# The tanh that ends a state convolution, written into the convolution's PSUM bank instead of an SBUF tile

## What is computed

```
z, xbc, dt_raw, q, k, v, g_ssd, g_att = split_cols(u @ w_in.astype(u.dtype), IN_WIDTHS)
xbc = jax.nn.silu(causal_dwconv(xbc, conv_w, conv_b))
xs, bm, cm = split_cols(xbc, (SSD_INNER, SSD_GROUPS * SSD_STATE, SSD_GROUPS * SSD_STATE))
...
lmat = jnp.exp(jnp.where(causal, cs_t[..., :, None] - cs_t[..., None, :], -jnp.inf))
cb = jnp.einsum('bclgn,bcsgn->bcgls', cc, bc)
y_diag = jnp.einsum('bcgls,bcgrls,bcsgrp->bclgrp', cb, lmat, xdt)
```

## Time and profile before

| | |
|---|---|
| median of 3 runs | 1600.13 us (1599.84 to 1602.13) |
| the profiled execution | 1600.18 us |
| its span, first to last instruction | 1598.4 us |
| TensorE busy | 1579.8 us, 99% |
| VectorE busy | 1130.6 us, 71% |
| ScalarE busy | 921.4 us, 58% |
| GpSimd busy | 153.7 us, 10% |

### The profile page before, as it was taken

How to read it: one execution, slowest core, us unless ns; L and a number is a source line. 1 busy time by engine, 2 the same in 40 slices (tenths; PEclk the granted TensorE clock), 3 DMA queues, 4 the chain that set the end, 5 groups by cost and what they waited for, 6 DMA issues and landing times.

```text
span 1598.4 us, 31022 instructions
## 1 busy us (share of the span) xinstructions
PE 1579.8 (99%) x12570; PEld 1542.4 (96%) x12570; DVE 1130.6 (71%) x2416; ACT 921.4 (58%) x1988; POOL 153.7 (10%) x162
## 2 busy tenths in 40 slices
PE   9999999999999999999999999999999999999998
PEld 9999999999999999999999999999999999999986
DVE  7554578787655888557458875597549997888862
ACT  5444356475443765447557544466776887567653
POOL 4000000000000000000000000102343752100000
PEclk9999999999999999999999999999999999999999
DMA  9554555555555555564265555654354335555551
GB/s 290 178 172 158 185 171 164 180 159 172 165 172 183 172 173 178 173 196 141 82 198 165 179 176 185 189 170 133 109 182 144 121 122 170 172 185 185 185 184 53
DMA packets 251390, 266.52 MB, mean 167 GB/s; under 512 B 4763, under 2 KB 246753, under 8 KB 251248
## 3 DMA queue, kind: packets, MB, share of 16 engines
q1 hardware_dynamic: 249600, 260.72, 51.2%
q0 software_dynamic: 1648, 3.81, 0.9%
HBM read 263.42 MB, written 1.09 MB: 165 GB/s over the span
## 4 chain that ended last, share of the span: by engine, by line
PE 85%; DVE 8%; ACT 5%; issue 1%; DMA 0%; SPq 0%; DVEq 0%; ACTq 0%
PE ps L1023 51%; PE ps L1025 25%; DVE wl L2188 3%; ACT wh L1482 1%; PE ps L988 1%; PE ps L986 1%; PE ps L987 1%; PE ps L778 1%; DVE CY L2154 0%; PE ps L763 0%; DVE CY L2276 0%; ACT YH L1328 0%; PE ps L796 0%; DVE R L1808 0%; DVE YB L2166 0%
## 5 line engine op out<-in xcount | busy, mean ns | idle before, releaser
L2188 DVE TENSOR_TENSOR wl<-raw,wh 128x512 fp32r<-128x512 f32 (+1 forms) x968 | 643.8, 715 | 277.0 <-ACT wh L1482 271.3
L1482 ACT ACTIVATE wh<-raw 128x512 fp32r<-128x512 f32 (+1 forms) x1004 | 551.4, 611 | 198.8 <-PE ps L1023 172.9
L1023 PE MATMUL ps<-XH,wh 128*128 128x258 f32 (+3 forms) x2464 | 617.0, 287 | 4.8 <-ACT XH L1118 3.5
L1025 PE MATMUL ps<-XH,wl 128*128 128x258 f32 (+3 forms) x2464 | 613.8, 285 | 0.0
L1023 PEld LDWEIGHTS ps<-XH,wh 128*128 128x128 f32 x2464 | 465.9, 189 | 8.4 <-issue 5.7
L1025 PEld LDWEIGHTS ps<-XH,wl 128*128 128x128 f32 x2464 | 465.2, 189 | 0.1
L1023 PE MATMUL ps<-XL,wh 128*128 128x258 f32 (+3 forms) x2464 | 333.7, 287 | 0.6 <-DVE XL L1891 0.6
L1023 PEld LDWEIGHTS ps<-XL,wh 128*128 128x128 f32 x2464 | 315.1, 189 | 1.8 <-DVE XL L1891 1.3
L1025 PE MATMUL ps<-HH,wl 128*128 128x272 f32 (+1 forms) x704 | 173.4, 284 | 0.0
L1023 PE MATMUL ps<-HH,wh 128*128 128x272 f32 (+1 forms) x704 | 173.4, 285 | 0.0
L1025 PEld LDWEIGHTS ps<-HH,wl 128*128 128x128 f32 x704 | 132.5, 188 | 0.0
(11 more groups left out here) (444 smaller groups left out, 2038.0 us busy)
## 6 DMA issues: line engine op xcount, KB each, us to landing
raw<-in_ffn_wg SPq DMA_DIRECT2D x44, 1024.0 KB, 5.4
raw<-in_ffn_wu SPq DMA_DIRECT2D x44, 1024.0 KB, 5.4
raw<-in_w_in SPq DMA_DIRECT2D x33, 1024.0 KB, 5.3
raw<-in_ffn_wd SPq DMA_DIRECT2D x32, 1024.0 KB, 5.2
raw<-in_w_ffn_in SPq DMA_DIRECT2D x22, 1024.0 KB, 5.1
raw<-in_ffn_wd SPq DMA_DIRECT2D x16, 768.0 KB, 4.6
raw<-in_conv_w_in SPq DMA_DIRECT2D x12, 1024.0 KB, 5.1
raw<-in_w_ffn_out SPq DMA_DIRECT2D x11, 1024.0 KB, 5.0
```

Of the source, the lines that this page charges most:

```text
L1023: mm = e.matmul(o, hi[:, k, c], xk, start=begin, stop=stop)
L1025: e.matmul(o, lo[:, k, c], xk, start=False, stop=False)
L1482: e.activation(wh[u.n % NH][:, c], raw[u.n % NR][:, c], ACT.Copy).then_inc(s_hi, 1)
L2188: e.tensor_tensor(wl[u.n % NR][:, c], raw[u.n % NR][:, c], wh[u.n % NH][:, c].bitcast(F32), ALU.subtract).then_inc(s_lo, 1)
```

## The change

For the eight groups xs (q from 4 to 11) the tanh goes into the PSUM bank of the group's own convolution, and the conv end reads it from there; q from 0 to 3 keep `TH`. The banks of xs j are therefore free only after the conv end: `free` names `s_cz` in place of `s_ctap`. ACT's wait for a free `TH` buffer is gone for these groups. On ACT, the tanh of xs j + 1 moves to the front of its even head step, ahead of EX; on DVE, the conv end moves up by two places in its step.

```diff
--- before.py
+++ after.py
@@ -558,7 +558,7 @@
     gs_after = (6,)
     mixed = []
     for j in range(8):
-        P.group(("xs", j), W_IN, KD, X_0 + 256 * j, 2, two(s_ctap, 6 * (4 + j) + 4))
+        P.group(("xs", j), W_IN, KD, X_0 + 256 * j, 2, two(s_cz, 2 * (4 + j)))
         mixed.append(("xs", j))
         if j == 0:
             P.drain("cb")
@@ -614,6 +614,9 @@
     x_hid = [Xs(HH[f], HL[f], s_hh, s_hl, 22 * f, n0, T) for f, n0 in enumerate((0, 0, NMETA, NMETA))]
     x_ch, x_o = Xs(CH, CL, s_ch, s_cl, 0, 0, T), Xs(OH, OL, s_oh, s_ol, 0, NMETA, T)
     x_a, x_y = Xs(AH, AL, s_ah, s_al, 0, 0, NV), Xs(YH, YL, s_yh, s_yl, 0, 0, NV)
+
+    def conv_bank(q, m):
+        return TH[q % 2][:, m, :] if q < 4 else PS[groups["xs", q - 4].b0 + m][:, 0:T]
 
     def src3(ps, n, sl=None):
         return ps.rearrange("p (a c) -> p a c", a=n)
@@ -1298,11 +1301,11 @@
     def act_conv_end(e, q):
 
         dst = [BC[:, 2 * q + m, :] for m in range(2)] if q < 4 else [CY[(q - 4) % 4][:, m, :] for m in range(2)]
-        if q > 1:
+        if 1 < q < 4:
             e.wait_ge(s_cz, 2 * (q - 2) + 2)
         for m in range(2):
             e.wait_ge(s_ctap, 6 * q + 4 + m + 1)
-            e.activation(TH[q % 2][:, m, :], dst[m], ACT.Tanh, scale=0.5).then_inc(s_th, 1)
+            e.activation(conv_bank(q, m), dst[m], ACT.Tanh, scale=0.5).then_inc(s_th, 1)
 
     def act_gn(e, g, step):
 
@@ -1411,6 +1414,8 @@
 
     def act_heads(e):
         for c in range(16):
+            if c % 2 == 0 and c < 14:
+                act_conv_end(e, 5 + c // 2)
             yield
             E = EX[c % 2]
             if c > 1:
@@ -1424,10 +1429,7 @@
             e.wait_ge(s_er, c + 1)
             e.activation(E[:], E[:], ACT.Exp, scale=-1.0).then_inc(s_ee, 1)
             yield
-            if c % 2 == 0 and c < 14:
-                act_conv_end(e, 5 + c // 2)
-                yield
-                yield
+            yield from idle(2 * (c % 2 == 0 and c < 14))
             if c > 6:
                 if c != 14:
                     act_gn(e, (c - 7) // 4, (c - 7) % 4)
@@ -2100,11 +2102,11 @@
                             DTT[:, :, 2 * c:2 * c + 2].unsqueeze(3).to_broadcast([128, 3, 2, 64]),
                             ALU.mult).then_inc(s_xd, 1)
             yield
-            yield from idle(c % 2 == 0 and c < 14)
-            yield
             if c % 2 == 0 and c < 14:
                 dve_conv_end(e, 5 + c // 2)
                 yield
+            yield
+            yield from idle(c % 2 == 0 and c < 14)
             if c > 6:
                 if (c - 7) % 4 == 2:
                     dve_gn_add(e, (c - 7) // 4)
@@ -2151,7 +2153,7 @@
         dst = [BC[:, 2 * q + m, :] for m in range(2)] if q < 4 else [CY[(q - 4) % 4][:, m, :] for m in range(2)]
         for m in range(2):
             e.wait_ge(s_th, 2 * q + m + 1)
-            e.scalar_tensor_tensor(out=dst[m], in0=TH[q % 2][:, m, :], scalar=1.0, in1=dst[m], op0=ALU.add,
+            e.scalar_tensor_tensor(out=dst[m], in0=conv_bank(q, m), scalar=1.0, in1=dst[m], op0=ALU.add,
                                    op1=ALU.mult).then_inc(s_cz, 1)
 
     def dve_gn_add(e, g):
```

## The result

The changed kernel takes **1605.21 us** (median of 7 runs, 1603.89 to 1607.03), the kernel before 1600.32 (7 runs, 1599.84 to 1602.13) on the same chip: ratio 1.003, 95% interval 1.002 to 1.0039, which leaves out no change. The span of the profiled execution is 1603.6 us, 5.2 more than before's.

A forecast was written before the change was run, and what follows sets the result against it. TensorE, busy 99% of the span, was taken as the bound. The bank wait's +3.7 us less 0.55 us back gave +3.2 us (rounded up) on 1600.18, so 1603.4 us, range 1600.6 to 1607.0.

The forecast's parts named there:

- The bank wait: PE's first matmul of xs 7 waits for xs 6's conv end: 1285.0 instead of 1281.29, 3.7 us lost.
- the 3 to 4.5 named as the sign: Sign of being right: PE idle 3 to 4.5 us before xs 7's first matmul, released by the conv end.
- ACT's turn of 9.54 us: ACT's time from one group's first step CY to the next's, against PE's 9.1 us a group.
- Conv-end pair 0.84 us: On DVE, a conv-end pair reading PSUM takes 0.84 us instead of 1.33 (xs 6) or 2.00 (xs 1).
- The tanh into PSUM at nothing: Sixteen ACT tanh writing PSUM, -0.05 to +0.16 us apiece, counted as no change from 0.41 us each.
- ACT's pace: Before xs 7, ACT's longer turn costs PE up to a quarter microsecond a turn; not added, swallowed by the wait.
- 0.55 us back at step 12: PE, arriving 3.7 us later, finds YB of step 11 ready, so the 0.55 us wait before 1299.11 goes.
- the clock: Rival: PE's clock falls to 1.2 GHz at xs 7, costing 1 to 8 us, 3 taken, 1606.4 us; chance 0.12.
- the forecast case: The main outcome for the whole kernel, +2.2 to +4.4 us around 3.2; chance 0.55.
- the prediction's own signs: PE idle 3 to 4.5 us before xs 7 meant right; wait under 2 us or low clock behind it, wrong.
- ACT's order costs more: Rival: dearer tanh or late POOL masks make PE wait behind xs 7 too, 1604.5 to 1607 us; chance 0.13.
- DVE's relief opens the bank in time: Rival: lighter DVE opens xs 6's bank at 1281.5 to 1283.5, 0 to 2 us lost; chance 0.20.

The follow-up runs named there:

- e1: Changed kernel, but the tanh of xs 6 goes to SBUF and its banks are free after the taps; 1601.30 us.
- e6: Changed kernel with the conv end of xs 6 one low half earlier on DVE; 1603.72 us.
- e7: Changed kernel with the conv end of xs 6 two low halves later on DVE; 1610.19 us.
- e3: Changed kernel with ACT and DVE back in the order of before; tanh in the bank and all holds kept; 1604.67 us.
- e5: Kernel before, its order kept, with tanh in the bank held to the conv end for all xs groups but xs 6; 1598.88 us.
- e4: Changed kernel's order on ACT and DVE alone: tanh in SBUF, every bank free after the taps; 1601.29 us.
- e2: Changed kernel with 16 matmuls into unused columns while PE waits for the banks of xs 6; 1603.69 us.
- e9: The changed kernel measured once more with no edit; 1605.63 us.
- e8: Changed kernel with the conv end of xs 6 one low half earlier and 8 unused matmuls inside PE's wait at xs 7; 1602.70 us.

## Why the prediction was right in its mechanism and low by 1.8 us

- *The bank wait, +3.7 us at xs 7, PE at 1285.0.* Right: 1285.50, 4.2 us later than before. The taps came 0.4 us later than forecast, 0.22 of it with the start of the stage; the low half ahead of the conv end held it up by 0.89 (1283.73 to 1284.62) and not 0.8. PE's wait itself reads 2.91, just under the 3 to 4.5 named as the sign, since PE arrived 1.3 us late (1285.50 - 2.91 = 1282.59, not 1281.29); e1 shows that this hold makes the loss, e6 and e7 that the conv end's place on DVE sets it.
- *ACT's turn of 9.54 us, first step of xs 6 at 1276.3, taps at 1278.8.* 1276.25 and 1279.23; from 1238.31 to 1276.25 there are four turns of 9.49. Right.
- *Conv-end pair 0.84 us, tanh 0.41.* 0.78 and 0.40. The reason given, one operand in PSUM, is right by e3 and e5, but in the changed kernel the order does the same by itself (e4), which the prediction hadn't seen. The Trainium skill, "GPSIMD Engine Reference", Key points, says that GpSimd shares its SBUF interfaces with VectorE and gets in conflict with its instructions that have two SBUF inputs; e3 against before agrees, 0.78 against 2.33 us beside POOL.
- *The tanh into PSUM at nothing.* 12 ns each, 0.2 us for sixteen. The Trainium skill, "ScalarE: Activation LUTs", Step-by-step: what each stage is for, has ScalarE faster towards PSUM; the trace agrees, 402 against 414 ns. No run shows that it bought time.
- *ACT's pace costs PE up to ¼ us a turn before xs 7, swallowed by the bank wait.* Right in sum, wrong in shape: with the 0.22 us of the start of the stage taken off, y of step 4 is 0.9 us later than before, and no wait follows up to xs 7. But PE waits 0.31 at step 2, less than before, then 1.27 at once at step 4. On DVE's timeline YB of step 3, for which y of step 4 waits, stands behind a pair of low halves that waited for ACT's high halves:

```profile
1254.71 2.43 DVE L2190 TENSOR_TENSOR wl<-raw,wh 128x512 fp32r<-128x512 f32 x2 [0.66 <-ACT wh L1484]
1257.07 0.47 DVE L2181 SCALAR_TENSOR_TENSOR YB<-CY,DC,ps 128x258 f32<-128x258 f32 x1
```

  Right that it is swallowed: the bank's opening hangs on ACT and DVE. Where the hold is gone (e1, e4) the wait at step 4 stays, and the kernel is 1 us over before, as the medians have it.
- *0.55 us back at step 12, none at the squares' sums.* 0.6 and none. Right.
- *The sum.* This is the step that was off: the clock stood among the rivals at 0.12 and 3 us instead of in the sum. It cost 1.6 us in the profile and 1.5 by e2, in 12 of 13 executions by their time and clock. +3.2 and 1.6 make +4.8; the medians differ by +4.9. The rows of before couldn't tell its price, but a wait that the forecast itself makes three times longer than any in the trace was reason to put the fall into the forecast case, at the low end of the 1 to 8 us. By the prediction's own signs the wait at the bank spoke for it and the low clock behind xs 7 against it. The measured +4.9 us lies above its forecast case of +2.2 to +4.4 and in the part that it had given to the slower rivals; the range holds it because of them.
- *ACT's order costs more.* It didn't: no wait on YB stands behind xs 7, both lie at steps 2 and 4. Its range, 1604.5 to 1607, holds the measured time by chance.
- *DVE's relief opens the bank in time.* It fell. With the order of before the relief does bring the bank's opening to 1283.53 (e3), the late end of the 1281.5 to 1283.5 that this rival named; PE still waits 3.7 us, because the same relief brings PE there sooner.

## What to carry to other kernels

Holding a buffer for longer costs little where the hold still ends before the next user starts, and nearly everything where it ends after. So list for each hold the time between its new end and the next user's start, and leave out the hold where that is negative: here one pair of banks of eight made 3.9 of 4.9 us, and leaving it out in the old order gave the fastest kernel. When a forecast makes the tensor engine wait longer than it has waited anywhere in the trace, put a loss of clock behind that wait into the sum. Before you credit a new operand place with a shorter instruction, ask whether a change of order has moved that instruction out of its neighbour's way.

## What the runs showed of the hardware

The granted clock fell from 2.4 to 1.2 GHz behind PE waits of 3.68 us (in e3's profile), of 2.91 and 2.90 us (in those of the changed kernel and of e9) and of 2.01 us (in e6's profile, and by their times in six of its eleven executions). In the changed kernel's profile it fell 0.6 us after PE had started again, in e3's and e6's 1.2 to 1.3 us after, in e9's about as PE started; in e7, with 6.04 us of waiting, it had fallen already. The Trainium skill, "TensorE: Matmul & The Clock Gate", Why this matters for your kernels, tells one to keep PE's idle gaps under about 3 us; the trace of e6 differs, with a fall behind 2.01 us, and the measurement decides.

The profiled execution of e9 was one of the high ones (1607.07 us), and its windows show a second fall, far from the change:

```profile
1072.00:1075.00 3.00, 2.15 (x18) 1.71 (x17) 3.00 (x8) 1.41 (x3) 0.00 (x0) 1.00 0.66 227
1075.00:1079.00 4.00, 4.00 (x20) 3.82 (x20) 2.43 (x5) 0.56 (x3) 0.00 (x0) 0.57 0.00 0
1079.00:1081.00 2.00, 2.00 (x18) 2.00 (x17) 0.79 (x2) 0.65 (x2) 0.00 (x0) 1.00 0.00 0
```

What precedes it on PE is a wait of 0.85 us and then narrow matmuls:

```profile
1073.09 0.41 PE L878 MATMUL ps<-DTA,tri 128*128 128x32 f32 x2 [0.85 <-DVE DTA L2053]
1073.34 0.39 PE L879 MATMUL ps<-DTA,tri 128*128 128x32 f32 x2
```

e8's profile, another high one, has the fall there as well, behind 0.83 us of wait. The profiled execution of the changed kernel has 0.81 us of wait at the same place and that of before 0.86, and both have a clock of 1.00 from 1072 to 1081. So behind a far shorter wait, with narrow matmuls after it, the clock falls in some executions of a kernel and not in others, and the length of the wait alone does not decide it: e9's high execution is 2 us above the three at 1605.0. That this is also what lifts some of before's executions to 1602 us is likely by their clock of 0.998, but none of those was profiled. What decides between the two in a single execution stays open.
